# Hymba layer on eight cores: the conv shuffle by way of a DRAM scratch, and four changes of order

## What is computed

```python
h = rms_norm(x, pre_norm_g)
p = h @ w_in + b_in
q, k, v, g_attn, glu_val, glu_gate, g_conv = split(p, SPLIT_POINTS)
q = partial_rope(q, cos, sin); k = partial_rope(k, cos, sin)
attn = sliding_window_attention(q, k, v, sinks) * silu(g_attn)
c = depthwise_conv31(glu_val * sigmoid(glu_gate)) + b_dw
conv = (silu(layer_norm(c)) @ w_pw + b_pw) * silu(g_conv)
y = concat([attn, conv]) @ w_out + b_out
out = x + rms_norm(y, post_norm_g)
```

## Time and profile before

| | before |
|---|---|
| median of 3 runs | 1096.62 us (1094.29 to 1097.99) |
| profiled execution, device time | 1096.66 us |
| its span, slowest core (core 2) | 1095.1 us |
| spans of the eight cores | 1081.7 to 1095.1 us |
| PE / DVE / ACT / POOL busy, core 2 | 94 / 48 / 38 / 19% of the span |
| DMA, core 2 | 141.94 MB, mean 130 GB/s |

### The profile page before, as it was taken

One profiled execution on the slowest core, in us unless ns is written; L12 is line 12 of the kernel. 1 busy time (PEld: TensorE's weight loads), 2 busy tenths in 40 slices (PEclk: granted clock), 3 DMA queues, 4 the chain that ended last, 5 costly groups with the idle time before them and its releaser, 6 DMA issues.

```text
span 1095.1 us, 18077 instructions; the slowest of 8 cores (1081.7 to 1095.1 us)
## 1 busy us (share of the span) xinstructions
PE 1033.6 (94%) x7002; PEld 552.5 (50%) x7002; DVE 526.3 (48%) x921; ACT 414.1 (38%) x1015; POOL 211.2 (19%) x216
## 2 busy tenths in 40 slices
PE   5998999999999999999999999989999999999997
PEld 3884444555555444445544644456555644444443
DVE  5554201556556275356645640046676627433434
ACT  5341223465554444044411212264656544402111
POOL 1340000235434410000000000013454441000000
PEclk9999999999999999999999999999999999999999
DMA  8944434355566589968499313356455747992435
GB/s 217 275 97 71 78 57 77 99 118 132 128 133 164 137 201 158 213 184 208 85 158 174 77 28 59 72 112 158 118 134 135 192 96 183 174 171 39 83 75 113
DMA packets 26678, 141.94 MB, mean 130 GB/s; under 512 B 6001, under 2 KB 6385, under 8 KB 16241
## 3 DMA queue, kind: packets, MB, share of 16 engines
q0 software_dynamic: 8928, 80.74, 42.6%
q1 hardware_dynamic: 17666, 60.04, 17.2%
HBM read 171.72 MB, written 32.51 MB: 186 GB/s over the span
## 4 chain that ended last, share of the span: by engine, by line
PE 70%; DMA 9%; SPq 8%; DVE 6%; ACT 4%; issue 2%; POOL 1%; ACTq 0%; DVEq 0%; POOLq 0%
PE psum L1271 19%; PE psum L902 10%; PE psum L1150 10%; SPq L152 8%; DMA arena<-arena 6%; PE psum L664 5%; PE psum L1240 5%; PE psum L996 4%; PE psum L955 3%; PE psum L945 3%; ACT arena L1055 2%; PE psum L660 2%; DMA arena<-w_in 2%; PE psum L1309 1%; PE psum L622 1%
## 5 line engine op out<-in xcount | busy, mean ns | idle before, releaser
L1271 PE MATMUL psum<-arena 128*128 128x512 bf16 x960 | 208.8, 379 | 0.0
L1271 PEld LDWEIGHTS psum<-arena 128*128 128x128 bf16 x960 | 93.6, 98 | 111.4
L955 PE MATMUL psum<-arena 128*128 128x352 bf16 (+1 forms) x768 | 120.7, 310 | 3.5 <-ACT arena L958 3.5
L945 PE MATMUL psum<-arena 128*128 128x352 bf16 (+1 forms) x768 | 122.9, 314 | 0.0
L1055 ACT ACTIVATE arena<-psum,arena 128x128 f32<-128x128 f32 x256 | 94.1, 368 | 61.4 <-DVE arena L1045 43.3
L1150 PE MATMUL psum<-arena 128*128 128x512 bf16 x512 | 112.2, 379 | 3.6 <-ACT arena L1154 3.0
L902 PE MATMUL psum<-arena 128*128 128x512 bf16 x512 | 112.5, 383 | 0.0
L955 PEld LDWEIGHTS psum<-arena 128*128 128x128 bf16 x768 | 74.7, 98 | 42.9 <-issue 5.7
L945 PEld LDWEIGHTS psum<-arena 128*128 128x128 bf16 x768 | 71.9, 98 | 46.8 <-issue 12.7
L1034 DVE COPY_PREDICATED psum<-arena,psum 128x1024 f32<-128x1024 uint16 x32 | 38.7, 1208 | 116.1 <-PE psum L1028 116.1
L1069 POOL TENSOR_TENSOR arena<-arena 128x1024 bf16<-128x1024 f32 x32 | 60.6, 1893 | 140.3 <-DVE arena L1068 140.3
(11 more groups left out here) (148 smaller groups left out, 1287.8 us busy)
## 6 DMA issues: line engine op xcount, KB each, us to landing
arena<-w_in POOLq DMA_DIRECT2D x12, 2048.0 KB, 15.2
arena<-x_ext SPq DMA_DIRECT2D x18, 1024.0 KB, 11.0
arena<-w_in POOLq DMA_DIRECT2D x15, 1024.0 KB, 11.3
out<-arena POOLq DMA_DIRECT2D x15, 1024.0 KB, 8.7
arena<-w_out POOLq DMA_DIRECT2D x6, 2048.0 KB, 19.6
arena<-arena SPq DMA_DIRECT2D x64, 66.0 KB, 2.0
arena<-arena SPq DMA_DIRECT2D x64, 65.9 KB, 2.0
arena<-arena SPq DMA_DIRECT2D x64, 65.9 KB, 2.0
```

Of the source, the lines that this page charges most:

```text
L945: cx.op('pe', lambda e, k=k: e.matmul(out=bank[bv][:, 0:n], lhsT=wbuf.ap[:, k, o:o + 128], rhs=xv[:, k, st:st + n], start=(k == 0), stop=( ...
L955: cx.op('pe', lambda e, k=k: e.matmul(out=bank[bg][:, 0:n], lhsT=wbuf.ap[:, k, o + 128:o + 256], rhs=xv[:, k, st:st + n], start=(k == 0), ...
L1271: cx.op('pe', lambda e, k=k: e.matmul(out=bank[b], lhsT=MIX.ap[:, k, j * 128:(j + 1) * 128], rhs=wo[n][k][0].ap[:, wo[n][k][1], :], start= ...
```

## The change

Five edits. (1) conv_shuffle no longer copies within SBUF: conv_store(c) writes hglu[c % 2] to one of two DRAM scratch slots with one DMA as soon as the GLU part is done, and four DMAs read it back, one per shift, each with all four channel groups; they wait for the store's semaphore, and as before for the taps of c - 1. (2) drain() moves into the gate loop, behind the first group's products and Silu. (3) SEQ_B becomes two strings: KT and KE of tiles 6 and 7 move from the end of SEQ_A to behind q_a of tile 1, and KT and KE of tile 8 from there to behind q_a of tile 2. (4) In the norm stage products rotate over all eight banks, and ln_chunk is called in pairs so that the last one precedes the last gconv. (5) The opening: the first x tile is SP's first load, the k/v weights wait for this tile and no longer for the second, and in SEQ_A three q transposes (QT) move behind other PE work (QT.0 behind B.4, QT.1 behind QA.4, QT.2 behind B.5).

```diff
-KE.2 QA.3 KV.3 QB.0 K1.3 SQ.4 QB.1 QF.0 K2.3 QR.0 N.4 QB.2 QF.1 SQ.5 QT.0 B.4 QR.1 QF.2 K3.3 QB.3
-Eb.4 Ea.4 N.5 QR.2 QT.1 QE.0 KT.3 QA.4 QE.1 KE.3 SQ.6 QF.3 QT.2 B.5 QR.3 QB.4 Eb.5 Ea.5 N.6 QE.2
+KE.2 QA.3 KV.3 QB.0 K1.3 SQ.4 QB.1 QF.0 K2.3 QR.0 N.4 QB.2 QF.1 SQ.5 B.4 QT.0 QE.0 QR.1 QF.2 K3.3
+QB.3 Eb.4 Ea.4 N.5 QR.2 KT.3 QA.4 QT.1 QE.1 KE.3 SQ.6 QF.3 B.5 QT.2 QR.3 QB.4 Eb.5 Ea.5 N.6 QE.2
...
-KV.6 QE.7 K1.5 K2.5 KT.4 K3.5 KE.4 KV.7 K1.6 K2.6 KT.5 K1.7 KE.5 KV.8 K3.6 K2.7 K3.7 KT.6 K1.8 KE.6
-KT.7 KE.7
+KV.6 QE.7 K1.5 K2.5 KT.4 K3.5 KE.4 KV.7 K1.6 K2.6 KT.5 K1.7 KE.5 KV.8 K3.6 K2.7 K3.7 K1.8
 """
-SEQ_B = "K2.8 K3.8 KT.8 KE.8"
+SEQ_B = ("KT.6 KE.6 KT.7 KE.7 K2.8 K3.8", "KT.8 KE.8")
...
+        scr = nc.dram_tensor("scr", [2, 128, HW], BF16, kind="Internal").ap()
...
+                p1_load(0, 1, 0, bufs)
                 cx.dma('sp', grow.ap[0:1, :], gpre_d[0:1, :], s_gpre, W=[grow], nowait=True)
...
-                for n in range(3):
+                for n in (1, 2):
...
-                    cx.dma('pool', kvh[h].ap, wv(w_in, 1024, 256, 8 * h, 8), sem, R=[bufs[0][1]], W=[kvh[h]])
+                    cx.dma('pool', kvh[h].ap, wv(w_in, 1024, 256, 8 * h, 8), sem, R=[bufs[0][0]], W=[kvh[h]])
...
-                if s == 0 and j == 1:
-                    play(SEQ_B)
+                if s == 0 and j < 3:
+                    play(SEQ_B[j - 1])
                 later(lambda j=j, b_=b_: q_b(1, j, b_))
-            drain()
...
                         bias=cp[:, C_BGA + c:C_BGA + c + 1]), R=[BK[b], cpa], W=[gateA[c]])
+                    drain()
...
+            def conv_store(c):
+                cx.dma('sp', scr[c % 2], hglu[c % 2].ap, s_ss[c % 2], R=[hglu[c % 2]], W=[scr_t[c % 2]])
+
             def conv_shuffle(c):
-                hg = hglu[c % 2]
-                for g in range(4):
-                    for i in range(4):
-                        cx.dma('sp', rs.ap[32 * i:32 * (i + 1), g, 0:HW - i], hg.ap[32 * g:32 * (g + 1), i:HW],
-                               s_rs, R=[hg], W=[rs], group=True)
+                for i in range(4):
+                    cx.dma('sp', rs.ap[32 * i:32 * (i + 1), :, 0:HW - i],
+                           scr[c % 2].rearrange("(g p) n -> p g n", p=32)[:, :, i:HW], s_rs, R=[scr_t[c % 2]], W=[rs], group=True)
...
                 glu_fin(c)
+                make_diag(c)
+                conv_store(c)
                 tick()
...
+            rot["list"] = list(range(8))
             for c in range(3, 8):
                 gconv(c)
...
-                if c == 3:
-                    ln_chunk(2)
-                    ln_chunk(3)
-                else:
-                    if c < 8:
-                        ln_chunk(c)
+                for c_ in ((2, 3), (4, 5), (6,), (7,), ())[c - 3]:
+                    ln_chunk(c_)
```

More of the change, by code:

```diff
@@ L386, in build_program @@
         s_x4 = cx.dsem("xr4")
+        s_ss = [cx.dsem("ss%d" % i) for i in range(2)]
+        scr = nc.dram_tensor("scr", [2, 128, HW], BF16, kind="Internal").ap()
+        scr_t = [T("scr%d" % i) for i in range(2)]
         s_rs = cx.dsem("rs")
@@ L976, in glu_fin, with make_diag @@
                     cx.op('pool', lambda e: e.tensor_copy(out=hg.ap[:, 0:32], in_=tail.ap[:, c, :]), R=[tail], W=[hg])
+            def make_diag(c):
                 dg = diag[c % 2]
@@ L1138, in superblock @@
                 conv_shuffle(c)
+                tick()
                 if c < (NJ if s + 1 < NSUP else NJ - 1):
@@ L1142, in superblock @@
                            group=True)
-                tick()
             def gconv(c):
```

## The result

The changed kernel takes **1083.56 us** (median of 4 runs, 1083.40 to 1083.86), beside a median of 1096.62 for the kernel before on the same chip; the ratio is 0.9884, 95% interval [0.9863, 0.9905]. The forecast was 1076.0 in a range from 1069 to 1086: the direction is right and the range holds, but of 20.6 us only 13.1 came, and the result lies outside the band from 1071 to 1079 that was given a chance of 0.60. The profiled execution of the changed kernel took 1083.86 us.

What follows compares the result with a forecast made beforehand. The prediction took PE's work plus its waits as the bound. Common gains of 5.9 + 4.1 + 5.2 + 1.3 = 16.5 us and core 1's 0.3 left 1074.4, plus 1.6 outside the span: 1076.0 us, range 1069 to 1086.

Steps and rivals of the forecast that it cites:

- one of its own signs: Listed signs of being wrong: taps waiting for scratch reads, new PE waits replacing old, or opening over 2 us later.
- the sum for core 2: Whole span of core 2: 1095.1 less 16.5 common to all cores and 8.5 for the shuffle, giving 1070.1 us.
- Conv shuffle: Conv taps: fewer SP issues end PE's waits for shuffle DMAs; 8.5 us gained on core 2, 0.3 on core 1.
- (a): Conv taps: DMA engines, not SP's issuing, limit, so core 2 keeps its waits; 1080.2 us, chance 0.15.
- (c): Conv taps: DRAM round trip exceeds its window, decisive above 14.9 us landing; at worst 1142 us, chance 0.05.
- Drain and SEQ_B: q and gates: rope waits 2.09 us per superblock, slow gates 1.68; k-copy wait and slow q products 4.1; all gone.
- Norm stage: gconv and pointwise: PE's waits for Silu bank release and last layer-norm Silu go; 5.2 us over both superblocks.
- Second superblock: The drain's 2.09 us rope wait and the norm stage's waits, expected to go here as in the first superblock.
- Opening: First loads and q transposes: 1.3 us gained, bounds 4.8 us lost to 5.3 gained.
- by 26 us most of the delay lies where PE waited for weights anyway, about 1.5 us of it is left: Opening: of a 4.8 us delay from the gain row landing with the first tile, about 1.5 us remains.
- rival (b): Opening: gain row lands with the first tile and the whole 4.8 us reaches q; 1082.1 us, chance 0.15.

Runs made afterwards that it cites:

- e4: The kernel before with the shuffle through DRAM and nothing else; 1092.60 us, ratio 0.9956 to the kernel before.
- e5: The changed kernel with the old shuffle of 16 on-chip copies; 1084.92 us, ratio 0.9899 to the kernel before.
- e9: e8 with the second superblock's gain rows and first x tiles no longer held until w_out's third quarter has landed; 1076.01 us, ratio 0.9812.
- e8: The changed kernel with all first loads as before and the second query weights issued three POOL ropes earlier; 1079.52 us, ratio 0.9848.
- e2: The changed kernel with only gain row, positions and constants back ahead of the first x tile, k/v weights still early; 1081.49 us, ratio 0.9860.
- e1: The changed kernel with all first loads as before, k/v weights again waiting for the second tile; 1080.21 us, ratio 0.9848.
- e3: The changed kernel with only the second query weights' load issued three POOL ropes earlier; 1082.10 us, ratio 0.9860.

## Why the prediction was right and where it was wrong

The time lies in the range, but by one of its own signs the prediction is wrong: the opening ends later than before by more than 2 us, 2.7 in the median and 7.6 from core 2 before to core 0 after. By its steps, from the slowest core before (core 2) to the slowest after (core 0), 12.8 us less where the sum for core 2 had 25.0:

- **Conv shuffle, 8.5 us: right.** The stage fell from 143.0 to 135.4 us, 7.6, and to the same value on all cores. That core 1 would leave only part of it is shown by e4. In the changed kernel its worth in time is not shown: taking it back cost 1.4 us, within the noise (e5). Rivals (a) and (c) are out: no core's taps wait for the loads, and the median store and last load take 2.1 and 5.8 us on core 1, 2.1 and 7.7 on core 3, the slowest, together under the 14.9 at which they would have decided.
- **Drain and SEQ_B, in the first superblock 2.09 + 1.68 + 4.1 = 7.9 us: right in size,** by the stages; no run takes these two edits back alone. Second half of q and gates together went from 36.0 + 96.9 to 32.1 + 93.8 us, 7.0 less. Two things that the sum did not have are in this, and partly cancel by luck: core 0 has the new slow stretch, and it lacks an old one that some cores have among the first GLU products (16 products of L945 take 4.24 us at 201 us on core 2 before, 2.56 in the changed kernel on core 0). With the old one and without the new one, on core 0 of e9, it is 29.3 + 95.5, 8.1 less.
- **Norm stage, 2.6 us in each superblock: the waits went as said** (2.9 us in gconv and pointwise), but the step left out what is late next. The second superblock's x tiles wait for a quarter of w_out, which came no sooner (on core 1 the DMA that waits for it is issued 89.4 us after the first gconv product before and 89.8 in the changed kernel); their transposes then waited in the output stage, which grew by 1.7 us. e9 shows the cause in e8's setting; on the changed kernel itself the hold was not taken away.
- **Second superblock, 2.09 + 2.6 = 4.7 us: right**, 520.2 to 515.6.
- **Opening, 1.3 us gained: wrong in sign, by 8.9 us.** The failed step is "by 26 us most of the delay lies where PE waited for weights anyway, about 1.5 us of it is left". At 26 us it was so on some cores only. The wait for the second part of the k/v weights, 0.9 to 1.6 us before, is gone on all eight. On core 4 the 48 products run through and are done at 28.7 us, where core 2 was done at 31.0 before; but on core 0 they start at 26.23 and end at 32.5.

```profile
23.28 5.40 PE L784 MATMUL psum<-arena 128*128 128x256 bf16 x48
```

Behind them stands the fourth tile, and its load shares full queues with the weights that were now asked for 6 us earlier: the tile is squared at 26.4 to 27.6 us with the early weights (e2) and at 22.9 to 24.2 without them (e1). The DMA share is about 1.0 from 10 to 35 us in both kernels (0.94 to 1.06 in each 5 us, cores 0 and 2 before, 0 and 4 after), so what one transfer gains another loses. Nor was the gain row alone late, as rival (b) had it: the constants that DVE's tables wait for came behind it, at 9.70. And the sum named no one who would be hit by a later opening; it was the load that stands behind POOL's rope, and the rope itself became longer.

Rival (b), 1082.1 us, came closest. The late start that it names is half of what happened, as e1 and e2 show; the weights that then land too late it did not name. With the old first loads, the earlier weights and the freed tiles (e9) the kernel takes 1076.01 us. The sum without its opening gives 1077.3, so the rest of it stands in the main; that the two lie so close is partly luck, since e9 has two gains that the sum did not count.

## What to carry to other kernels

Where the DMA queues are full, a load put first is a load put before another: follow the delay to the last load of the stretch and to each DMA issue that stands in an engine's program order behind late work. An issue whose buffer is free belongs where the queues are idle, not where the text of the program happens to come to it. And a gain on one stage's path is kept only if the loads that feed the next stage start earlier by as much; the time of the slowest of eight cores shows that only when the last such wait is gone (e3 gained nothing over the changed kernel and e8 nothing over e1; e9 is 3.5 us below e8).

## What the runs showed of the hardware

I had taken it that small loads issued behind the 1 MB tile land with it. On core 0 of the changed kernel the gain row (8 KB) was there at 6.50 us and the tile's square began at 7.43, but the positions, issued at 1.86, landed 7.5 us later, at 9.4, and the constants at 9.70; before, the positions took 1.7 us (core 2).

```profile
7.43 1.91 ACT L526 ACTIVATE arena<-arena 128x2048 bf16<-128x2048 f32 x1 [4.53 <-DMA arena<-x_ext]
```

```profile
arena<-pos_t SPq DMA_DIRECT2D x1, 8.5 KB, 7.5
```

An issue on SP has no fixed price: 0.43 us each for the four loads of 264 KB from DRAM (1.72 / 4), 0.45 to 0.58 for sixteen of 66 KB from DRAM, 0.61 to 0.80 for sixteen of 66 KB from on-chip to on-chip (9.79 to 12.85 / 16).
